# Second phase of a hybrid decoder step: each block's recurrence cut into 27 stages, rounds that mix the stages of neighbouring blocks

## The chip, the cores and the metric

One core of a Trainium2 chip. The metric is the device time of one launch in microseconds (us), the median of the runs shown. Engine names: PE is TensorE (PEld its weight loads), DVE is VectorE, ACT is ScalarE, POOL is GpSimd, SP is the queue that issues the weight DMAs.

## The reference, cut to what matters

One layer of a decoder, for a prompt of 1024 tokens and 8 single-token samples, width 1024. A normed and modulated input goes through `w_in`; three recurrences run side by side on its columns, then `w_out`, a second norm and a SwiGLU network.

```
mod = silu(c) @ w_ada + b_ada                      # sh1, sc1, g1, sh2, sc2, g2
h = rmsnorm(x) * (1 + sc1) + sh1
proj = h @ w_in                                    # HGRN2 | Mamba-2 | RWKV-7 columns
o_hg: S_t = diag(f_t) S_{t-1} + k_t v_t^T, o_t = S_t^T q_t ; rmsnorm per head, * silu(gate)
y_mb: h_t = exp(dt A) h_{t-1} + dt x_t B_t^T, y_t = h_t C_t ; + D x, * silu(z), rmsnorm
o_rw: RWKV-7
x = x + g1 * (concat(o_hg, y_mb, o_rw) @ w_out)
h = rmsnorm(x) * (1 + sc2) + sh2
x = x + g2 * ((silu(h @ w_gate) * (h @ w_up)) @ w_down);  y = rmsnorm(x)
```

Both chunked recurrences must carry a state from one block of 128 tokens to the next.

## The kernel before

There are three stretches. The first phase does the input norm, `w_in` and RWKV-7. The **second phase** runs HGRN2 and Mamba-2 over eight blocks of 128 tokens. The rest is the feed-forward network, with the samples' states in between. Every engine runs its own program, and all programs are written out from one list, `PLAN2` (built around lines 816 to 1010): each item names a piece of work, and each engine does its part of the items in the list's order. An engine never reorders, so a wait in one item holds up all that stands behind it on that engine. Semaphores count finished steps; `step(names, name, b)` gives the count at which step `name` of block `b` is done.

Per block the second phase has these pieces. HGRN2: `hg_logits` (DVE takes the negative magnitude, ACT exp and log), `hg_gate`, `hg_low`, `hg_high` (DVE builds the gates' running sums and differences over 5 levels, ACT exponentiates them), `hg_levels` (DVE multiplies them with keys and queries), `hg_att` (PE transposes, then 192 small matmuls, L1697; DVE masks and adds, `HAS`, `HAT`, `HAD`; ACT copies values, `HVD`), `hg_state` (PE L1705, DVE carries the state, `HSH`, L3008), `hg_o` (PE L1713 and L1718), `hg_sq` (DVE copies and squares, `HT`, PE sums, L1724, ACT inverse root), `hg_out`. Mamba-2: `mb_turn` (PE transposes and two products, DVE `XD`, `CBM`), `mb_decay` (PE running sums, L1754, ACT exp `E2`, DVE 8 subtractions `SEG`, L3088, ACT exp, L2322, DVE `MM`, L3093; POOL scales `XDE` and `CE`), `mb_prod` (PE L1766, L1769, L1772; DVE `YS`, the state `STt`, the gate), `mb_sq` (ACT square, PE sum, L1782, ACT inverse root), `mb_out`.

All of a block's pieces come one after the other, in one fixed order for all blocks, and one item carries the piece's work of all engines. Only `hg_logits`, `hg_gate`, `hg_low`, `hg_high`, `mb_turn`, `hg_levels` of block b+1 are set among the pieces of block b. Between pieces stands work that fills PE:

- in blocks 0 to 2 one quantum of `ada` (8 small matmuls on a 512 KB piece of `w_ada`, L1377; 32 quanta in all), with three transposes of the input, `hg_x`;
- in blocks 3 to 7 dense quanta: one is the product of a 128-wide weight tile with 384 tokens, 24 matmuls (three per contraction tile, L1346 to L1348, high and low parts), or about half of that for `down`. `FILL` puts up to two halves, mostly a whole quantum, behind each of six pieces. Quanta 110 to 117 are the output projection, then comes the second norm (`sum`, `scaled`, `head`, `rest`), and 118 to 139 are gate, up and down of the network. Each needs its weights loaded (SP, three `RAW` buffers), cast on ACT (L1959) and its remainder formed on POOL (L1093), for two slots.

After block 7 come the transposes of the remaining input (`x`), a meeting of all engines (`mark`, `join`), and the network at full pace. All of the work is one stream: what the second phase has not done of the dense quanta is done after it.

Of the kernel before, what the change touches and what calls it, by code (L numbers as in the profile page):

```python
# [39 lines left out]
P = 128  # L40
# [59 lines left out]
HGF_DVE = ['nabs', 'logf', 'diffs', 'factors']  # L100
# [4 lines left out]
MBF_DVE = ['xdt', 'cb']  # L105
MB_DVE = ['seg', 'm', 'y', 'S', 'z', 'out']
MB_PE = ['acum', 'y', 'S', 'ssq']
MB_ACT = ['E2', 'L', 'squared', 'rs']
# [62 lines left out]
def kernel_program(nc, ins, outs):  # L171
# [84 lines left out]
    with ctx:  # L256
# [354 lines left out]
        xb_act = sem("xb_act")  # L611
        hgf_dve = sem("hgf_dve")
        hgf_act = sem("hgf_act")
        mbf_dve = sem("mbf_dve")
        mbf_pe = sem("mbf_pe")
        hg_dve = sem("hg_dve")
# [103 lines left out]

        def XUSE(i):

            return (i - 9) // 2 + 1
# [62 lines left out]
        for b in range(NB):  # L786
            for n, at in (('turn1', b), ('mean', b - 1), ('turn2', b), ('var', b - 1), ('mix', b + 1), ('inv1', b),
# [3 lines left out]
                if 0 <= at < NB:  # L791
# [4 lines left out]
                 'inv2': [('fin_shift', 0)], 'inv3': [('fin_conv', 0), ('hg_logits', 0)], 'inv4': [('pre', 'nabs')],  # L796
# [35 lines left out]
        for item in rw_end:  # L832
# [11 lines left out]
        NOW = {('out', (0, KT - 1)): [('sum', 3), ('pause', 0), ('scaled', (3, 0)), ('scaled', (3, 1)), ('head', 3),  # L844
                                      ('pause', 0), ('rest', (3, 0)), ('rest', (3, 1)), ('pause', 0)]}
# [65 lines left out]
        FILL = {'hg_att': 2, 'mb_decay': 2, 'hg_o': 2, 'mb_prod': 2, 'mb_turn': 2, 'hg_levels': 2}  # L911
        for b in range(NB):
            items = [('hg_att', b), ('hg_state', b), ('mb_decay', b), ('hg_o', b), ('hg_logits', b + 1), ('mb_prod', b),
                     ('hg_sq', b), ('hg_gate', b + 1), ('hg_low', b + 1), ('hg_high', b + 1), ('mb_turn', b + 1), ('mb_sq', b), ('hg_out', b),
                     ('hg_levels', b + 1), ('mb_out', b), ('hg_x', b)]
            for item in items:
                if item[1] == NB or (item[0] == 'hg_x' and b > 2):
                    continue
                PLAN2.append(item)
                if item == ('hg_att', 0):  # L920
                    PLAN2.append(('mb_turn', 0))
                if b > 2:
                    fill(FILL.get(item[0], 0))
                elif item[0] not in ('hg_logits', 'hg_gate', 'hg_low', 'hg_out', 'hg_x') and late:
                    group, part, half = UNITS[QUANTA[late[0]][0]][1]
                    if (part, half) == (0, 0) and group > 1:
                        PLAN2.append(('adt', group - 1))
                    PLAN2.append(('mm', late.pop(0)))
                    if not late:
                        PLAN2.append(('adt', 2))  # L930
# [74 lines left out]
        def _(pool):  # L1005
# [122 lines left out]
            def mb_decay(b):  # L1128
                pool.wait_ge(mbf_dve, step(MBF_DVE, 'xdt', b))
                g.tensor_tensor(XDE[:, :, :], XD[:, :, :], ES[:, b, :].unsqueeze(2).broadcast_to([P, 8, 64]),  # L1130
                                ALU.mult).then_inc(mb_pool, 1)
                pool.wait_ge(mb_act, step(MB_ACT, 'E2', b))
                g.tensor_tensor(CE[:, :, :], E2[:, :, :], XB[5][:, b * BLK:(b + 1) * BLK].unsqueeze(1).broadcast_to([P, 4, P]),
                                ALU.mult).then_inc(mb_pool, 1)
# [31 lines left out]
            for what, arg in PLAN2:  # L1166
                if what == 'mb_decay':
# [110 lines left out]
        def _(pe):  # L1278
# [5 lines left out]
            def turn_x(i, bufs):  # L1284

                b0 = 3 + 2 * (i % 2) if i < 9 else 0
# [11 lines left out]
                for k in range(KT):  # L1298
                    src = bufs[i] if i < 9 else bufs[(i - 9) % 2]
                    last = turn(BK8[b0 + k // 4][:, (k % 4) * P:(k % 4) * P + n], src[0:n, k * P:(k + 1) * P], n)  # L1300
                last.then_inc(x_turned, 1)

            def dense(q, half=None):
# [13 lines left out]
                if q >= QJ and (PREV[q] is None or PREV[q] < QP2):  # L1317
                    pe.wait_ge(x_act, 18)
                    pe.wait_ge(x_dve, 18)
                if c == chunks(u)[0] and half != 1:  # L1320
                    pe.wait_ge(w_hi, SIDX[u] + 1)
                    pe.wait_ge(w_lo, SIDX[u] + 1)
# [344 lines left out]
            def hg(stage, b):  # L1667
# [7 lines left out]
                if stage == 'att':  # L1675
# [3 lines left out]
                    if 0 < b <= 3:  # L1679
                        pe.wait_ge(x_act, 9 + b)  # L1680
                        pe.wait_ge(x_dve, 9 + b)
# [5 lines left out]

# [34 lines left out]
                elif stage == 'sq':  # L1722
# [3 lines left out]
                elif stage == 'x':  # L1726
                    pe.wait_ge(*V('out'))
                    pe.wait_ge(mb_act, step(MB_ACT, 'rs', b))
                    turn_x(9 + b, XTOK2)

            def mb(stage, b):
# [19 lines left out]
                elif stage == 'decay':  # L1751
# [4 lines left out]
                    last.then_inc(mb_pe, 1)  # L1756
                elif stage == 'prod':
                    pe.wait_ge(*V('m'))
# [16 lines left out]
                elif stage == 'sq':  # L1775
# [161 lines left out]
        def _(act):  # L1937
# [65 lines left out]
            def x_half(i, dst, t0):  # L2003
                act.wait_ge(x_turned, i + 1)
                n = BLK if i % 9 < NB else NS
                b0 = 3 + 2 * (i % 2) if i < 9 else 0
                a.copy(dst[:, 0:4, t0:t0 + n], BK8[b0][:, :].rearrange("p (k t) -> p k t", k=4)[:, :, 0:n]).then_inc(
# [49 lines left out]
            def ffn_step(what, arg):  # L2057
# [11 lines left out]
                elif what == 'mixsplit':  # L2069
                    if arg == 0:  # L2070
                        act.wait_ge(ada_turned, 3)
# [176 lines left out]
            def hg(stage, b):  # L2248
# [6 lines left out]
                if stage == 'logits':  # L2255
                    act.wait_ge(hgf_dve, step(HGF_DVE, 'nabs', b))
# [10 lines left out]
                elif stage == 'att':  # L2267
# [10 lines left out]
                elif stage == 'sq':  # L2278
# [29 lines left out]
            def mb(stage, b):  # L2308
# [6 lines left out]
                if stage == 'decay':  # L2315
                    act.wait_ge(*T_('acum'))
# [3 lines left out]
                    last.then_inc(mb_act, 1)  # L2320
                    act.wait_ge(*V('seg'))
                    a.activation(SEG[:, :, :], SEG[:, :, :], ACT.Exp).then_inc(mb_act, 1)  # L2322
                elif stage == 'sq':
                    act.wait_ge(*V('z'))
                    a.activation(T4[:, :, :], YS[:, :, :], ACT.Square).then_inc(mb_act, 1)
                    act.wait_ge(*T_('ssq'))
# [60 lines left out]
            for what, arg in PLAN2:  # L2387
                if what == 'adt':
# [40 lines left out]
        def _(dve):  # L2429
# [88 lines left out]
            def x_half(i, dst, t0):  # L2518
                dve.wait_ge(x_turned, i + 1)
                n = BLK if i % 9 < NB else NS  # L2520
                b0 = 3 + 2 * (i % 2) if i < 9 else 0
                v.tensor_copy(dst[:, 4:8, t0:t0 + n],
                              BK8[b0 + 1][:, :].rearrange("p (k t) -> p k t", k=4)[:, :, 0:n]).then_inc(x_dve, 1)
# [415 lines left out]
            def hg(stage, b):  # L2939
# [11 lines left out]
                if stage == 'logits':  # L2951
                    dve.wait_ge(hg_loaded[b % 2], 16 * (b // 2 + 1))
                    hg_nabs(HN, HB).then_inc(hgf_dve, 1)
# [30 lines left out]
                elif stage == 'att':  # L2984
# [28 lines left out]
                elif stage == 'sq':  # L3013
# [50 lines left out]
            def mb(stage, b):  # L3064
# [11 lines left out]
                if stage == 'turn':  # L3076
                    dve.wait_ge(mbf_pe, b + 1)
# [7 lines left out]
                elif stage == 'decay':  # L3085
                    dve.wait_ge(*A('E2'))
# [3 lines left out]
                    last.then_inc(mb_dve, 1)  # L3090
                    dve.wait_ge(*A('L'))
# [3 lines left out]
                    last.then_inc(mb_dve, 1)  # L3095
                elif stage == 'prod':
                    dve.wait_ge(*T_('y'))
                    mb_skip(YS, lambda t: XB[t][:, cols], lambda t: (M1, M2)[t // 2][:, (t % 2) * P:(t % 2 + 1) * P]).then_inc(mb_dve, 1)
                    dve.wait_ge(*T_('S'))
# [4 lines left out]
                    dve.wait_ge(*V('y'))  # L3104
                    v.tensor_tensor(YS[:, :, :], YS[:, :, :], MIX[:, 2:6, cols], ALU.mult).then_inc(mb_dve, 1)
# [127 lines left out]
            for what, arg in PLAN2:  # L3233
                if what == 'adt':
# [55 lines left out]
```

## Time and profile before

| | |
|---|---|
| time, median of 3 runs | 1798.88 us (1790.7 to 1802.05) |
| profiled execution: span from first to last instruction | 1790.1 us |
| PE, DVE, ACT busy | 89%, 58%, 37% |
| second phase, 609.33 to 979.00 us | 369.67 us, PE busy 289.51 us, granted clock 0.82 |
| network, 1100 to 1790 us | PE busy 95%, granted clock 0.99 |

The profiled execution's own device time isn't on the page; its span lies 0.6 us below the fastest of the three runs. Times within the trace are counted from the span's start. The granted clock is a share of 2.4 GHz, the mean over a stretch.

### The profile page before, as it was taken

The page shows a single profiled execution, that of the slowest core. Times are in us where ns is not written, and L with a number is a line of the kernel's source. Part 1 is how long each engine was busy: PE and PEld are TensorE (multiplying, and loading weights), DVE is VectorE, ACT ScalarE, POOL GpSimd, SP SyncE. Part 2 cuts the span into 40 slices and gives each one's busy share as a digit, 9 for nine tenths or more (in the row PEclk, how much of TensorE's full clock was granted, in tenths as well). Part 3 has the DMA queues.
Part 4 walks back from the last instruction along what each step waited for, and adds up shares of the span by engine and source line. Part 5 has one row for each costly group of instructions (what it writes and reads, how often), then busy time and mean ns, then how long its engine had stood idle before and what let it go on. Part 6 is the DMA issues. An engine that isn't in the chain of part 4 may idle for free.

```text
span 1790.1 us, 32642 instructions
## 1 busy us (share of the span) xinstructions
PE 1594.7 (89%) x13639; PEld 1451.0 (81%) x13639; DVE 1043.3 (58%) x2152; ACT 660.4 (37%) x1133; POOL 249.0 (14%) x331
## 2 busy tenths in 40 slices
PE   4799999889999677777888899989899999999997
PEld 2798888778887443575777899988899999999997
DVE  5513456868554556676765254676665566655554
ACT  2323333223432322343433254343544444433333
POOL 4421111111111200231334300100000000000000
PEclk9899999889999667897998999999999999999999
DMA  8111001101112244321132434544464544564552
GB/s 320 53 48 36 25 25 37 44 33 50 49 43 106 80 164 151 110 86 34 42 89 71 136 117 130 151 121 138 119 200 137 160 122 139 152 176 137 145 151 75
DMA packets 276684, 188.09 MB, mean 105 GB/s; under 512 B 7880, under 2 KB 264377, under 8 KB 275513
## 3 DMA queue, kind: packets, MB, share of 16 engines
q1 hardware_dynamic: 266050, 160.28, 29.8%
q0 software_dynamic: 7536, 22.47, 3.8%
q10 hardware_dynamic: 2950, 3.24, 0.5%
q8 instruction: 109, 1.79, 0.4%
q14 instruction: 39, 0.31, 0.1%
HBM read 172.82 MB, written 13.18 MB: 104 GB/s over the span
## 4 chain that ended last, share of the span: by engine, by line
PE 70%; DVE 17%; ACT 7%; issue 3%; DMA 1%; SPq 0%; POOL 0%; DVEq 0%; ACTq 0%; POOLq 0%
PE bank L1346 16%; PE bank L1347 16%; PE bank L1348 16%; PE bank L1282 3%; PE bank L1368 3%; PE bank L1369 2%; ACT WHI L1959 2%; PE bank L1370 2%; DVE WLO L2442 1%; PE bank L1512 1%; PE bank L1520 1%; PE bank L1522 1%; PE bank L1697 1%; PE bank L1456 1%; PE bank L1377 1%
## 5 line engine op out<-in xcount | busy, mean ns | idle before, releaser
L2442 DVE TENSOR_TENSOR WLO<-RAW,WHI 128x1024 fp32r<-128x1024 f32 (+4 forms) x235 | 247.1, 1052 | 265.1 <-ACT WHI L1959 263.3
L1959 ACT CAST WHI<-RAW 128x1024 fp32r<-128x1024 f32 (+4 forms) x294 | 266.4, 910 | 227.6 <-PE bank L1348 201.0
L1346 PE MATMUL bank<-HAH,WHI 128*128 128x384 f32 (+1 forms) x832 | 277.2, 333 | 12.4 <-DVE HAL L2625 5.9
L1347 PE MATMUL bank<-HAL,WHI 128*128 128x384 f32 (+1 forms) x832 | 273.7, 329 | 0.0
L1348 PE MATMUL bank<-HAH,WLO 128*128 128x384 f32 (+1 forms) x832 | 273.0, 328 | 0.0
L1346 PE MATMUL bank<-MIXR,WHI 128*128 128x384 f32 (+2 forms) x528 | 174.1, 330 | 12.6 <-DVE MIXR L2572 3.8
L1093 POOL TENSOR_TENSOR WLO<-RAW,WHI 128x1024 fp32r<-128x1024 f32 (+1 forms) x59 | 124.6, 2114 | 434.7 <-ACT WHI L1959 434.7
L1346 PEld LDWEIGHTS bank<-HAH,WHI 128*128 128x128 f32 x832 | 159.9, 192 | 16.3 <-issue 15.5
L1347 PE MATMUL bank<-MIXR,WHI 128*128 128x384 f32 (+2 forms) x528 | 171.1, 324 | 0.0
L1348 PE MATMUL bank<-MIXR,WLO 128*128 128x384 f32 (+2 forms) x528 | 171.1, 324 | 0.0
L1347 PEld LDWEIGHTS bank<-HAL,WHI 128*128 128x128 f32 x832 | 159.9, 192 | 0.1
L1348 PEld LDWEIGHTS bank<-HAH,WLO 128*128 128x128 f32 x832 | 159.7, 192 | 0.0
L1346 PE MATMUL bank<-HBH,WHI 128*128 128x320 f32 x416 | 132.2, 318 | 11.2 <-DVE WLO L2442 10.5
L1348 PE MATMUL bank<-HBH,WLO 128*128 128x320 f32 x416 | 129.7, 312 | 0.0
L1347 PE MATMUL bank<-HBL,WHI 128*128 128x320 f32 x416 | 129.6, 312 | 0.0
L1346 PE MATMUL bank<-HHI,WHI 128*128 128x344 f32 x344 | 114.7, 333 | 11.2 <-DVE HLO L2661 7.1
L1346 PEld LDWEIGHTS bank<-MIXR,WHI 128*128 128x128 f32 x528 | 101.4, 192 | 16.7 <-issue 13.8
L1347 PE MATMUL bank<-HLO,WHI 128*128 128x344 f32 x344 | 111.4, 324 | 0.0
L1348 PE MATMUL bank<-HHI,WLO 128*128 128x344 f32 x344 | 111.4, 324 | 0.0
L1368 PE MATMUL bank<-HHI,WHI 128*128 128x344 f32 x280 | 104.6, 373 | 3.7 <-ACT STG L1992 3.7
L1347 PEld LDWEIGHTS bank<-MIXR,WHI 128*128 128x128 f32 x528 | 101.1, 191 | 0.2
L1348 PEld LDWEIGHTS bank<-MIXR,WLO 128*128 128x128 f32 x528 | 101.0, 191 | 0.0
(582 smaller groups left out, 3031.6 us busy)
## 6 DMA issues: line engine op xcount, KB each, us to landing
RAW<-in_w_gate SPq DMA_DIRECT2D x66, 512.0 KB, 3.8
RAW<-in_w_up SPq DMA_DIRECT2D x66, 512.0 KB, 3.8
RAW<-in_w_ada SPq DMA_DIRECT2D x32, 512.0 KB, 4.4
RAW<-in_w_in SPq DMA_DIRECT2D x26, 512.0 KB, 3.8
RAW<-in_w_out SPq DMA_DIRECT2D x24, 512.0 KB, 3.5
RAW<-in_w_down SPq DMA_DIRECT2D x32, 384.0 KB, 3.1
RAW<-in_w_down SPq DMA_DIRECT2D x32, 320.0 KB, 2.8
ADAW<-in_w_ada SPq DMA_DIRECT2D x8, 1024.0 KB, 19.8
```

The costliest lines, as they stand in the source:

```text
L1093: g.tensor_tensor(wlo[:, 0:nk, :], RAW[u % NRAW][:, 0:nk, :], whi[:, 0:nk, :].bitcast(F32), ALU.subtract).then_inc(w_lo, 1)
L1282: return nc.tensor.transpose(out, in_, ident[0:n, 0:n])
L1346: mm(bank[:, 0:w], whi[:, k, :], hi_k, start=(k == 0), stop=False)
L1347: mm(bank[:, 0:w], whi[:, k, :], lo_k, start=False, stop=False)
L1348: last = mm(bank[:, 0:w], wlo[:, k, :], hi_k, start=False, stop=(k == nk - 1))
L1368: mm(bank[:, 0:CH], whi[:, k, :], HHI[:, k, cols], start=(k == 0), stop=False)
L1369: mm(bank[:, 0:CH], whi[:, k, :], HLO[:, k, cols], start=False, stop=False)
L1370: last = mm(bank[:, 0:CH], wlo[:, k, :], HHI[:, k, cols], start=False, stop=(k == KT - 1))
L1377: return mm(bank[32 * a_:32 * a_ + 32, :], CT[:, k, :], w, start=(k == 0 and half == 0), stop=(k == KT - 1), skip_group_check=True)
L1456: mm(BK8[2 + v // 2][:, o:o + w], WL[:, j * P:(j + 1) * P], la[:, v, 0:w], start=True, stop=True)
L1959: a.copy(w_split(i)[0][:, 0:nk, :], RAW[u % NRAW][:, 0:nk, :]).then_inc(w_hi, 1)
L2442: v.tensor_tensor(wlo[:, 0:nk, :], RAW[u % NRAW][:, 0:nk, :], whi[:, 0:nk, :].bitcast(F32), ALU.subtract).then_inc(w_lo, 1)
```

## The change

The stages of a block are cut finer and get semaphores that let them be placed apart: `hg_att` becomes `turn`, `att`, `mask`; `hg_logits` becomes `nabs` and `soft`; `hg_sq` becomes `ho`, `ssq`, `rs`; `mb_turn` becomes `turn`, `xd`; `mb_decay` becomes `acum`, `seg`, `L`, `m`; `mb_prod` becomes `prod`, `y`, `S`; `mb_sq` becomes `sq`, `ssq`. That is 27 stages with the pieces that stay whole. An item's work on one engine thus no longer stands in front of what another item wants from it. Three lists give the order of a round: `AROUND` for blocks 0 to 2, with 13 places for an `ada` quantum, `NROUND` for block 4, with the second norm inside, and `FROUND` for the rest. A round holds stages of block b-1 (`mb_S`, `mb_ssq`, `hg_out`, `mb_out`), of b, of b+1 (`hg_gate`, `hg_low`, `hg_high`) and of b+2 (`hg_nabs`, `hg_soft`). Dense halves come mostly one at a time. The modulation's copy, turn and addition (`adc`, `adt`, `adm`) stand 4, 5 and 7 stages behind the last `ada` quantum of a group. The transposed input uses banks 2 and 7 instead of 0 and 1 for its first three tiles. The mixing of the first 384 tokens waits expressly for blocks 0 to 2.

By the two lists, the work between the sums of squares of neighbouring blocks (`mb_ssq`, L1782) holds, in whole dense quanta, 4 before and 2 after for block 3; 5 and 7.5 for block 4; 6 and 5 for block 5; 6 and 4.5 for block 6; 5 and 4 for block 7. When block 7 is through, quanta up to 139 are done before and up to 136 after. The following engines' meeting stands before quantum 156 in the old list and before quantum 150 in the new one.

```
-        FILL = {'hg_att': 2, 'mb_decay': 2, 'hg_o': 2, 'mb_prod': 2, 'mb_turn': 2, 'hg_levels': 2}
-        for b in range(NB):
-            items = [('hg_att', b), ('hg_state', b), ('mb_decay', b), ('hg_o', b), ('hg_logits', b + 1), ('mb_prod', b),
-                     ('hg_sq', b), ('hg_gate', b + 1), ('hg_low', b + 1), ('hg_high', b + 1), ('mb_turn', b + 1), ('mb_sq', b), ('hg_out', b),
-                     ('hg_levels', b + 1), ('mb_out', b), ('hg_x', b)]
...
+        AROUND = [('mb_ssq', -1), ('mb_S', -1), ('mb_turn', 0), ('hg_levels', 0), ('hg_turn', 0), ('ada', 0), ('hg_att', 0),
+                  ('ada', 0), ('mb_xd', 0), ('hg_out', -1), ('mb_out', -1), ('mb_acum', 0), ('ada', 0), ('ada', 0),
+                  ('hg_mask', 0), ('mb_seg', 0), ('mb_L', 0), ('hg_state', 0), ('hg_x', 0), ('ada', 0), ('ada', 0), ('ada', 0),
+                  ('mb_m', 0), ('hg_o', 0), ('hg_gate', 1), ('ada', 0), ('hg_low', 1), ('ada', 0), ('mb_prod', 0), ('hg_ho', 0),
+                  ('hg_ssq', 0), ('hg_high', 1), ('ada', 0), ('hg_rs', 0), ('hg_nabs', 2), ('mb_y', 0), ('mb_sq', 0),
+                  ('ada', 0), ('hg_soft', 2), ('ada', 0)]
+        FROUND = [('mb_S', -1), ('fill', 2), ('mb_ssq', -1), ('mb_turn', 0), ('hg_levels', 0), ('hg_turn', 0), ('hg_out', -1),
+                  ('mb_xd', 0), ('fill', 1), ('hg_att', 0), ('hg_mask', 0), ('mb_acum', 0), ('mb_seg', 0), ('hg_state', 0),
+                  ('mb_L', 0), ('mb_m', 0), ('mb_out', -1), ('fill', 3), ('hg_o', 0), ('hg_gate', 1), ('mb_prod', 0),
+                  ('hg_low', 1), ('hg_ho', 0), ('fill', 1), ('hg_high', 1), ('fill', 1), ('mb_y', 0), ('mb_sq', 0),
+                  ('hg_nabs', 2), ('fill', 1), ('fill', 1), ('hg_soft', 2), ('hg_ssq', 0), ('hg_rs', 0)]
+        NROUND = [('mb_ssq', -1), ('mb_S', -1), ('mb_turn', 0), ('hg_levels', 0), ('fill', 1), ('hg_turn', 0), ('fill', 1),
+                  ('mb_xd', 0), ('hg_att', 0), ('hg_out', -1), ('mb_out', -1), ('hg_mask', 0), ('mb_acum', 0), ('mb_seg', 0),
+                  ('mb_L', 0), ('hg_gate', 1), ('mb_m', 0), ('hg_state', 0), ('sum', 0), ('scaled', 0), ('hg_o', 0),
+                  ('scaled', 1), ('hg_low', 1), ('hg_ho', 0), ('mb_prod', 0), ('hg_ssq', 0), ('head', 0), ('hg_high', 1),
+                  ('rest', 0), ('rest', 1), ('hg_nabs', 2), ('mb_y', 0), ('go', 0), ('mb_sq', 0), ('hg_rs', 0), ('hg_soft', 2),
+                  ('fill', 1)]
...
+        for b in range(NB + 1):
+            for stage, ahead in (AROUND if b < 3 else NROUND if b == 4 else FROUND):
+                at = b + ahead
+                if stage == 'ada':
+                    ada_quantum()
+                elif stage == 'fill':
+                    if b < NB and ('mb_out', 2) in PLAN2:
+                        fill(ahead)
+                elif stage in ('sum', 'head'):
+                    fill(len(QUANTA))
+                    PLAN2.append((stage, 3))
```

## Rows read from the trace of the kernel before

**Rows 1.** The page: busy time by engine; clock in 40 slices (tenths).
```profile
PE 1594.7 (89%) x13639; PEld 1451.0 (81%) x13639; DVE 1043.3 (58%) x2152; ACT 660.4 (37%) x1133; POOL 249.0 (14%) x331
...
PEclk9899999889999667897998999999999999999999
```

**Rows 2.** Windows: from:to, length, busy us (instructions) of PE, PEld, DVE, ACT, POOL, clock.
```profile
609.33:979.00 369.67, 289.51 (x3434) 224.38 (x3434) 245.84 (x646) 130.80 (x230) 101.60 (x70) 0.82 0.31 97
```

**Rows 3.** Windows of the second phase's single rounds, and one of the network.
```profile
609.33:648.68 39.35, 30.90 (x420) 17.34 (x421) 25.25 (x80) 10.30 (x20) 9.88 (x15) 0.68 0.51 167
...
691.23:725.69 34.46, 26.49 (x408) 14.81 (x408) 23.58 (x78) 10.89 (x21) 3.21 (x3) 0.80 0.59 190
...
835.24:883.38 48.14, 42.46 (x460) 37.73 (x459) 34.42 (x83) 21.07 (x37) 16.83 (x9) 0.93 0.18 53
...
1060.00:1100.00 40.00, 39.66 (x236) 38.48 (x234) 19.91 (x32) 17.14 (x30) 0.00 (x0) 0.99 0.43 126
```

**Rows 4.** Timeline of PE: the sum of squares of all eight blocks, idle before it.
```profile
643.53 1.16 PE L1782 MATMUL bank<-T,ones 128*128 128x128 f32 x8 [1.29 <-ACT T L2325]
...
719.97 1.16 PE L1782 MATMUL bank<-T,ones 128*128 128x128 f32 x8 [0.44 <-ACT T L2325]
...
772.38 1.16 PE L1782 MATMUL bank<-T,ones 128*128 128x128 f32 x8 [3.53 <-ACT T L2325]
...
830.08 1.16 PE L1782 MATMUL bank<-T,ones 128*128 128x128 f32 x8 [1.72 <-ACT T L2325]
...
878.20 1.16 PE L1782 MATMUL bank<-T,ones 128*128 128x128 f32 x8 [3.46 <-ACT T L2325]
...
931.48 2.07 PE L1782 MATMUL bank<-T,ones 128*128 128x128 f32 x8 [4.89 <-ACT T L2325]
...
975.15 1.76 PE L1782 MATMUL bank<-T,ones 128*128 128x128 f32 x8 [3.50 <-ACT T L2325]
```

**Rows 5.** Chain that ended last, 640 to 743 us: start, us, what.
```profile
642.30 3.79 DMA RAW<-in_w_ada
...
700.71 2.17 DVE SEG L3088 x8
702.90 1.06 ACT SEG L2322
...
738.47 4.31 DVE HAL L2625
```

**Rows 6.** Timeline of PE: first dense matmul of the phase, and one 4 us later.
```profile
742.92 0.66 PE L1346 MATMUL bank<-HAH,WHI 128*128 128x384 f32 x1 [5.95 <-DVE HAL L2625]
...
744.02 0.52 PE L1346 MATMUL bank<-HAH,WHI 128*128 128x384 f32 x1
...
748.09 0.33 PE L1347 MATMUL bank<-HAL,WHI 128*128 128x384 f32 x1
```

**Rows 7.** Chain that ended last, second norm, 798 to 823 us.
```profile
800.06 2.38 DVE SSA L2589
...
806.08 4.33 DVE MIX L2546 x8
...
810.44 4.16 ACT HAH L2044 x8
...
814.63 4.32 DVE HAL L2560 x8
...
822.82 0.62 PE bank L1346
```

**Rows 8.** Waits from 609 to 979 us: total, times, longest.
```profile
ACT WHI L1959 <- PE bank L1348: 76.2, 20, 7.0
```

**Rows 9.** Timeline of ACT and DVE: a weight cast; one DVE operation twice.
```profile
847.26 1.04 ACT L1959 CAST WHI<-RAW 128x1024 fp32r<-128x1024 f32 x1 [6.98 <-PE bank L1348]
...
868.99 0.42 DVE L2922 TENSOR_TENSOR HK<-HF,HB 128x256 f32<-128x256 f32 x1
...
922.24 2.50 DVE L2922 TENSOR_TENSOR HK<-HF,HB 128x256 f32<-128x256 f32 x1
```

More of the change, by code:

```diff
@@ new lines, in kernel_program, with turn_group, ada_quantum @@
+        turning = []
+        def turn_group():
+            for due in turning:
+                due[0] -= 1
+            while turning and turning[0][0] <= 0:
+                PLAN2.append(turning.pop(0)[1])
+        def ada_quantum():
+            if late and not turning:
+                group, part, half = UNITS[QUANTA[late[0]][0]][1]
+                PLAN2.append(('mm', late.pop(0)))
+                if (part, half) == (KT - 1, 1):
+                    turning.extend([[4, ('adc', group)], [5, ('adt', group)], [7, ('adm', group)]])
@@ new lines, in kernel_program @@
+        PLAN2 += [('hg_nabs', 1), ('hg_soft', 1)]
+        for b in range(NB + 1):
[9 more added lines that the diff above has]
+                    PLAN2.append((stage, 3))
+                elif stage in ('scaled', 'rest'):
+                    PLAN2.append((stage, (3, ahead)))
+                elif stage == 'go':
+                    assert ffn[0][0] == 'stop', ffn[0]
+                    ffn.pop(0)
+                elif 0 <= at < NB and (stage, at) != ('hg_levels', 0):
+                    PLAN2.append((stage, at))
+                    turn_group()
@@ L931, in kernel_program @@
+        assert not turning
         assert not late
@@ L1319, in dense @@
                     pe.wait_ge(x_dve, 18)
+                if QP2 <= q < QJ and PREV[q] is None and half != 1:
+                    pe.wait_ge(x_act, 12)
+                    pe.wait_ge(x_dve, 12)
                 if c == chunks(u)[0] and half != 1:
@@ L1674, in hg @@
                 HB = HB2[b % 2]
-                if stage == 'att':
+                if stage == 'turn':
                     pe.wait_ge(hgf_dve, step(HGF_DVE, 'factors', b))
@@ L2266, in hg @@
                     a.activation(HD[:, :, :, :], HD[:, :, :, :], ACT.Exp).then_inc(hgf_act, 1)
-                elif stage == 'att':
+                elif stage == 'turn':
                     act.wait_ge(*T_('turned'))
@@ L2387, in _ @@
             for what, arg in PLAN2:
-                if what == 'adt':
+                if what == 'adc':
                     ada_act(arg)
```

121 lines of the change are left out of this document (57 added, 64 removed).

## The prediction

> **What bounds the kernel now.** I read the page first: PE is busy 89% of the span, no other engine over 58%, and the clock row shows where PE is not at its pace: it stands at 9 and 10 tenths in the last half, and dips to 6, 7 and 8 in slices 14 to 22 [rows 1]. That is the second phase. The windows put numbers to it: in its 369.67 us PE is busy 289.51, DVE 245.84, ACT 130.80, at a mean clock of 0.82 [rows 2]. The network's stretch beside it has PE busy 39.66 of 40 us at 0.99 [rows 3]. So the phase loses time twice: 369.67 - 289.51 = 80.2 us of idle PE, and busy time at a low clock; 289.51 x 0.82 = 237 us is what its work would take at full clock. No engine fills the phase; it is bound by handovers. The chain of waits shows them: DVE subtracts for 2.17 us, ACT exponentiates for 1.06, in turn, with PE waiting for the end of that [rows 5], and PE's wait before the sum of squares, up to 4.89 us, comes in each of the eight blocks [rows 4]. After 979 us nothing of this remains, so what the phase saves goes to the end of the span one for one, except for dense work that it leaves for later.
>
> The markers that I use are the sums of squares of the blocks [rows 4]. Up to block 2's: 719.97 - 609.33 = 110.6 us. Then 52.4, 57.7, 48.1, 53.3 and 43.7 us for blocks 3 to 7, which is 365.8 us in all.
>
> **Rounds 0 to 2 (`ada`).** Nothing is added or removed: the same instructions on each engine, plus a few semaphore steps, at nothing. What moves is the order. A round's PE time was 26.5 us at clock 0.80, in a round of 34.5; DVE's was 23.6 [rows 3]. In the new order the subtraction on DVE runs while PE has the state product and `ada` quanta; the products `mb_prod` come after `hg_o` and two more quanta, and the sums of squares of block b come in the next round, behind three quanta. Walking the list with the measured durations, the DVE stream runs without a hole from `mb_m` to `hg_nabs`, and PE's own time is the longer one. I take PE's 26.5 us plus 3.5 for what is left: one is the load of a `w_ada` piece, on which the chain once stood 3.79 us [rows 5], because 11 quanta a round now come in groups of up to three, and there are three `RAW` buffers. 3 x 30 = 90 us instead of 110.6. Bounds: 26.5 (no waits at all) and 34.5 (nothing gained) a round.
>
> **Round 3.** Dense work now starts only after `mb_out` of block 2, which stands late, some 20 us into DVE's round of 23.6. Then ACT casts 3072 columns (estimate 3.1 us, from 1.04 for 1024 [rows 9]) with DVE waiting for it, and DVE forms the remainder in 4.31 us [rows 5]; the express wait makes that a chain. 20 + 3.1 + 4.3 = 27.5, then two quanta. A quantum is 24 matmuls; 236 took 40 us [rows 3], so 4.1 us. Round 3: 36 us instead of 52.4, with 2 quanta done instead of 4. The first dense matmul, at 742.92 us before [rows 6], comes at about 609 + 90 + 28 = 727.
>
> **Round 4 (norm).** PE's recurrence work is what round 5 shows: 42.46 x 0.93 = 39.5 us at full clock [rows 3], less six quanta of 4.1, or 15 us. Before the norm stand some 9 of these and six quanta, 24.6; with 2 of waiting, 36 us. The norm is a chain: from the last squares at 799.5 to the end of the remainder at 814.63 + 4.32 it took 19.4 us [rows 7]; of that DVE's additions of 2.38 would be less without POOL beside them, and the 4.33, 4.16 and 4.32 stay. PE has only `hg_o`, `mb_prod` and `hg_ssq` under it, 6 us. I take 19, plus a quantum and a half behind it, 6: 61 us instead of 57.7, but with 7.5 quanta instead of 5. Nothing is gained on this chain, since no stage of it moves.
>
> **Rounds 5 to 7.** Work of 15 us plus 5, 4.5 and 4 quanta: 35.5, 33.5 and 31.4 at full clock. DVE had 34.4 us in round 5 [rows 3], with less in the others. I take 38, 36 and 33, that is 2 to 2.5 above PE's work, instead of 48.1, 53.3 and 43.7.
>
> **Sum.** 90 + 36 + 61 + 38 + 36 + 33 = 294 us instead of 365.8: 71.8 earlier. Three quanta less are done by then, 3 x 4.1 = 12.3 us that come after: 59.5. The walk leaves out two things that rows show. The first dense matmuls after a wait take 0.66 and 0.52 us, 0.33 later [rows 6], so the first quantum took some 6 instead of 4.1; one such start in each of five rounds is 9.5 us. And DVE takes 2.50 us for what takes 0.42 otherwise, when POOL forms a remainder at the same time [rows 9]: this stays, and once a round it now falls on the chain, since DVE has fewer holes: 2.1 x 2.4 = 5. 59.5 - 14.5 = **45 us**. What a sum like this misses lies on both sides: neither at all gives 59.5, and a further 2.5 us of waiting a round gives 25; 65 is the end above, with the ada rounds at 28. Span 1790.1 - 45 = 1745; the median stood 8.8 us above this span, and I keep that: 1798.9 - 45 = **1754 us**.
>
> The later meeting of all engines moves before quantum 150, with less PE work between mark and meeting (two quanta of `down`, 4 us at most). POOL's outputs were issued long before, so I cost it at nothing; if POOL or DVE is behind it costs what they are late by, at most some 3 us. The change of banks and the three modulation items are nothing by themselves: the 4 to 7 stages between them replace PE's and DVE's waits for one another.
>
> **A view from the other side.** Work at full clock: 237 - 12.3 = 225 us. The forecast gives the phase 369.7 - 12.3 - 45 = 312.4 us; at a mean clock of 0.85 PE would be busy 265 us and idle 47, of the 80 now. DVE's 246 us are 79% of it.
>
> **The rivals.**
>
> *The dense bursts are broken up and the clock falls (slower).* Now the dense work comes in whole quanta; after the change a half, 2 us, stands between small matmuls and waits, and the ada rounds, where PE works in pieces of 1 us, ran at 0.68 [rows 3]. Place: rounds 3 to 7. With 47 us idle the phase costs 225 / c + 47: at c = 0.85 it is the forecast, at 0.725 it equals the old 357.4 (the quanta set aside), and from there on it is a loss; at 0.68 it is 378, 21 us slower: 1820. Against it: PE's idle stretches get shorter by the same change, and the clock was higher in the rounds in which PE idled least (0.93 in round 5, with 42.46 of 48.14 busy [rows 3]). The Trainium skill has a rule that speaks for this rival (TensorE: Matmul & The Clock Gate, section "A second HAM failure mode: psum-queue depth-cycling"): where PE idles a little between groups of matmuls that go to different banks, the clock goes back and forth and throughput drops. By the rule the halves, which cycle through three banks, would bring such a drop; the trace doesn't decide it, for it has no round with single halves. Chance 0.08.
>
> *ACT's queue takes back half.* ACT stands in its weight casts waiting for PE to release a slot: 76.2 us over 20 waits, up to 7.0 [rows 8, 9]. Behind such a cast are now `hg_soft`, `mb_sq`, `hg_rs` of other blocks. If each of the 27 casts in the phase makes one stage late by its 1.04 us [rows 9], that is 28 us: a gain of 17, 1782. For it: the dense weights have two slots, before and after. Against it: a cast is released when PE ends the very half that stands before it. Chance 0.17.
>
> *The order doesn't bound it.* If the pace is set by the weight stream or by DVE once its holes are filled, the PE waits come back under other names; gain within 8 us, 1795. Against it: DVE busy 66% and ACT 35% of the phase [rows 2], and twice the pace of weights in the network, without PE waiting. Chance 0.07.
>
> **How the numbers follow.** Forecast (gain 25 to 65) 0.64, more than 65 0.04, ACT's queue 0.17 (gain 8 to 25), no effect 0.07, clock 0.08. The range leaves out what lies beyond 65, the clock's case and most of "no effect": 1734 to 1791. A difference below 1% (18 us) is about what a measurement of this kernel can't tell from none. Faster by more: 0.64 + 0.04 + 0.10 of ACT's case = 0.78. Within 1%: the rest of ACT's case, most of "no effect", a little of the clock's: 0.13. Slower: 0.09.
>
> **What would show it.** PE idle in the phase down from 80 to about 47 us; clock from 0.82 to about 0.85, most of it in rounds 0 to 2; sums of squares of blocks 2, 3, 4, 7 at about 699, 735, 796 and 903 us; the wait before them (3.5 us, [rows 4]) gone; the first dense matmul at 727; the chain of the norm as long as before. Wrong would be: ada rounds still 34 us or more, a clock under 0.75 in rounds 5 to 7, DVE waiting for PE in the middle of a round while a bank waits to be emptied, or a wait of PE at the meeting.

## The result, and the profile after

The changed kernel takes 1767.03 us (median; 1764.87 to 1776.19) against 1798.92 before. The ratio is 0.9845, interval 0.982 to 0.987: faster by 1.3 to 1.8%, 23 to 32 us. The profiled execution's span is 1764.4 us, 25.7 below the one before. The forecast was 1754 us, a gain of 45, in a range up to 1791.

The page of the changed kernel, first part and clock; the second phase is slices 14 to 21:

```profile
span 1764.4 us, 32641 instructions
...
PE 1586.9 (90%) x13639; PEld 1448.9 (82%) x13639; DVE 1056.0 (60%) x2154; ACT 659.9 (37%) x1133; POOL 247.0 (14%) x329
...
PEclk9899999888999679788898999999999999999998
```

The instructions are the same in number on PE; only their places differ. Windows of the changed kernel: the whole phase up to the last state's transposes, then rounds 0 to 2, round 3, round 4 in three pieces (up to the norm's last squares, the norm, behind it), rounds 5, 6 and 7. Columns as in [rows 2]; behind the clock stand the DMA engines' busy share and GB/s.

```profile
609.33:931.59 322.26, 268.75 (x3363) 210.27 (x3363) 251.62 (x650) 124.46 (x220) 95.78 (x65) 0.83 0.35 107
...
609.33:698.47 89.14, 75.53 (x1221) 45.52 (x1221) 66.42 (x222) 30.59 (x60) 16.30 (x21) 0.80 0.65 212
698.47:736.88 38.41, 29.95 (x368) 24.32 (x368) 31.65 (x80) 15.03 (x23) 11.86 (x6) 0.73 0.24 66
...
736.88:779.44 42.56, 34.89 (x382) 32.59 (x380) 34.97 (x67) 16.70 (x29) 18.78 (x10) 0.96 0.30 86
779.44:799.02 19.58, 11.74 (x80) 6.18 (x81) 14.98 (x33) 7.87 (x15) 2.34 (x1) 0.56 0.18 51
799.02:806.92 7.90, 7.90 (x36) 7.90 (x37) 6.32 (x23) 3.19 (x6) 0.70 (x1) 0.78 0.01 2
806.92:846.53 39.61, 36.19 (x437) 31.83 (x436) 31.37 (x70) 19.41 (x34) 16.16 (x9) 0.96 0.22 65
846.53:888.82 42.29, 38.43 (x425) 32.38 (x424) 33.24 (x89) 16.46 (x31) 12.23 (x10) 0.84 0.16 45
888.82:925.00 36.18, 33.07 (x412) 28.69 (x412) 27.32 (x61) 12.27 (x21) 14.25 (x8) 0.91 0.28 82
```

PE idles 322.26 - 268.75 = 53.5 us in the phase instead of 80.2 [rows 2], and the clock went from 0.82 to 0.83 only. PE's waits in the phase, before and after:

```profile
PE bank L1782 <- ACT T L2325: 21.1, 8, 4.9
PE bank L1724 <- DVE HT L3017: 13.4, 5, 9.0
PE bank L1766 <- DVE MM L3093: 9.2, 3, 3.1
PE bank L1697 <- ACT HKT L2270: 7.7, 4, 3.2
```

```profile
PE bank L1758 <- DVE HSH L3053: 7.0, 3, 4.2
PE bank L1423 <- DMA RAW<-in_w_ada: 6.1, 5, 2.3
PE bank L1326 <- DVE MIX L3105: 5.5, 1, 5.5
PE bank L1326 <- DVEq L688: 5.2, 1, 5.2
...
PE bank L1825 <- ACT T L2370: 2.0, 2, 1.5
PE bank L1809 <- DVE MM L3139: 1.5, 1, 1.5
```

The four waits that led the list, 51 us, are nearly gone: 3.5 us of them are left. What leads now are waits for a state, for a `w_ada` piece, for the last block's `MIX` at the phase's end, and the barrier at the phase's start, which was there before. The sums of squares (L1825 now; its wait of up to 4.89 us [rows 4] is gone in six of eight blocks):

```profile
698.47 1.16 PE L1825 MATMUL bank<-T,ones 128*128 128x128 f32 x8 [0.53 <-ACT T L2370]
...
736.88 1.05 PE L1825 MATMUL bank<-T,ones 128*128 128x128 f32 x8
...
806.92 1.05 PE L1825 MATMUL bank<-T,ones 128*128 128x128 f32 x8
...
925.00 1.05 PE L1825 MATMUL bank<-T,ones 128*128 128x128 f32 x8
931.59 0.69 PE L1326 MATMUL bank<-ident,STt 128*128 128x128 f32 x2 [5.53 <-DVE MIX L3105]
```

| block's sum of squares | before | forecast | after |
|---|---|---|---|
| 2 | 719.97 | 699 | 698.47 |
| 3 | 772.38 | 735 | 736.88 |
| 4 | 830.08 | 796 | 806.92 |
| 7 | 975.15 | 903 | 925.00 |

The transposes of the state came at 979.10 us before and come at 931.59: 47.5 us, less three quanta of 4.1 left over, 35.2 us. But the span is only 25.7 us shorter. 9.5 us are lost **after** the phase. From the transposes of the last input tile to the sum of the norm behind the first `down` groups, the kernel before took 1265.68 - 1019.37 = 246.3 us, the changed one 1241.42 - 974.45 = 267.0, with five `down` quanta more, each of half a quantum's size (10.3 us): 10.4 too many. PE's waits in the changed kernel at the end of that stretch:

```profile
1213.51 0.41 PE L1392 MATMUL bank<-MIXR,WHI 128*128 128x384 f32 x1 [2.59 <-DVE WLO L2488]
...
1227.89 0.39 PE L1392 MATMUL bank<-HBH,WHI 128*128 128x320 f32 x1 [3.19 <-DVE WLO L2488]
...
1241.42 1.65 PE L1441 MATMUL bank<-SSA,ones 128*128 128x384 f32 x2 [4.50 <-DVE SSA L2634]
```

The longest wait for squares there was 1.47 us before. DVE and ACT beside them:

```profile
1220.61 1.22 DVE L3239 TENSOR_TENSOR SB<-SB,SW 128x1024 f32<-128x1024 f32 x1
1221.87 1.23 DVE L3240 TENSOR_TENSOR SW<-SB,SV 128x1024 f32<-128x1024 f32 x1
1223.12 1.22 DVE L3241 TENSOR_REDUCE SY<-SW 128x16 f32<-128x1024 f32 x1
1224.38 0.62 DVE L2561 SCALAR_TENSOR_TENSOR XTA<-bank,MOD,XTA 128x384 f32<-128x384 f32 x1
```

```profile
1229.78 1.28 ACT L1989 ACT_TABLE_LOAD   x1
1233.35 0.27 ACT L2418 ACTIVATE SRSV<-bank,CST 128x16 f32<-128x16 f32 x1 [2.28 <-PE bank L1881]
1233.65 0.21 ACT L2420 ACTIVATE SRSV<-SRSV 128x16 f32<-128x16 f32 x1
1233.89 1.28 ACT L1989 ACT_TABLE_LOAD   x1
```

L3239 to L3241 and L2418 are steps of the samples' states (`sm4b`, `sr12`). Three of them stand 3.7 us in front of the emptying of a bank (`XTA`), behind `down` quanta that PE had got through in 2.1 us each; the other takes two table loads (1.28 us each) and a wait in front of a weight cast. The samples' steps are placed by counting dense work from the meeting on. The meeting moved from quantum 156 to 150, and all 37 steps moved with it.

### The profile page after: what moved, and what is told of

It is laid out like the page before. It is cut to its first block, busy times and chain, and to the rows that moved or that the text cites. A ratio compares the mean times of both kernels' runs of the same rounds, so it can differ in the third digit from the quotient of the medians.

```text
span 1764.4 us, 32641 instructions
## 1 busy us (share of the span) xinstructions
PE 1586.9 (90%) x13639; PEld 1448.9 (82%) x13639; DVE 1056.0 (60%) x2154; ACT 659.9 (37%) x1133; POOL 247.0 (14%) x329
## 4 chain that ended last, share of the span: by engine, by line
PE 69%; DVE 19%; ACT 5%; issue 4%; DMA 2%; SPq 0%; POOL 0%; DVEq 0%; ACTq 0%; POOLq 0%
PE bank L1392 16%; PE bank L1393 16%; PE bank L1394 16%; PE bank L1326 3%; PE bank L1414 3%; PE bank L1415 2%; PE bank L1416 2%; ACT WHI L2002 1%; DVE WLO L2488 1%; PE bank L1423 1%; PE bank L1558 1%; PE bank L1566 1%; DVE HD L3023 1%; PE bank L1568 1%; PE bank L1797 1%
## 5 line engine op out<-in xcount | busy, mean ns | idle before, releaser
L1392 PE MATMUL bank<-HAH,WHI 128*128 128x384 f32 (+1 forms) x832 | 275.9, 332 | 13.6 <-DVE HAL L2605 4.2
L1392 PE MATMUL bank<-HBH,WHI 128*128 128x320 f32 x416 | 132.9, 319 | 13.1 <-DVE WLO L2488 11.6
```

Source lines behind the costliest of these rows:

```text
L1392: mm(bank[:, 0:w], whi[:, k, :], hi_k, start=(k == 0), stop=False)
```

## The experiments

All are compared with the kernel before in alternating runs; the changed kernel's ratio is 0.9845. A run's difference from the changed kernel is taken from the ratios, times 1797 us. Single profiles scatter: the second phase starts between 605.6 and 612.8 us in them (610.31 in the changed kernel), and round 0 takes 29.6 to 35.2 us from there in kernels with the same order, at clocks from 0.60 to 0.87. So the medians decide, and profiles are read for stretches.

**Old order in rounds 0 to 2.**

```
+        AOLD = [('hg_turn', 0), ('hg_att', 0), ('hg_mask', 0), ('ada', 0), ('hg_state', 0), ('ada', 0), ('mb_acum', 0), ('mb_seg', 0),
+                ('mb_L', 0), ('mb_m', 0), ('ada', 0), ('hg_o', 0), ('ada', 0), ('hg_nabs', 1), ('hg_soft', 1), ('mb_prod', 0),
...
-            for stage, ahead in (AROUND if b < 3 else NROUND if b == 4 else FROUND):
+            for stage, ahead in (AOLD if b < 3 else NROUND if b == 4 else FROUND):
```

> Blocks 0 to 2 in the old order, written with the new stages (all stages of a block one after the other, one ada quantum between pieces); blocks 3 to 7 as changed. My theory: the ada rounds took 110.6 us up to block 2's sum of squares before and 89.1 after, because the handovers are covered there; with the old order they go back to about 110, and the kernel to 1767 + 21 = 1788 us. Rival: the gain of these rounds is not the order of the stages but the modulation's three items set apart and the banks of the transposed input, which stay: then it stays at 1767, within 5 us.

1793.78 us, ratio 0.9991 (0.9973 to 1.001): 26 us slower than the changed kernel. The rival (banks and the modulation's items) is out. The window up to block 2's sum of squares, and from PE's waits (sum, count, longest):

```profile
609.33:729.67 120.34, 87.58 (x1222) 49.50 (x1222) 71.51 (x234) 30.04 (x58) 16.30 (x21) 0.68 0.49 160
```

```profile
PE bank L1818 <- DVE MM L3148: 9.2, 3, 3.1
```

The wait for `MM` is back, in the same 9.2 us as before, and the clock falls from 0.80 to 0.68. The same matmuls keep PE busy 87.6 instead of 75.5 us, and from where the phase starts it idles 29.3 instead of 12.6. My rewriting isn't the old list to the letter (the last `ada` quanta bunch up): counted from where its phase starts, 612.79, it took 116.9 us where the kernel before took 110.6, so the 26 us are an upper value for the order; the profiles before and after put it at 22. The scatter doesn't hide this: counted in the same way, the twelve kernels with the new order (the changed one and eleven of the runs below) took 83.5 to 95.2 us for these three rounds.

**Old order in rounds 3 to 7.**

```
-            for stage, ahead in (AROUND if b < 3 else NROUND if b == 4 else FROUND):
+            for stage, ahead in (AROUND if b < 3 else FOLD0 + FOLD if b == 3 else FOLD if b < NB else []):
```

`FOLD` is the old order in the new stages with `('fill', 2)` behind each piece; the norm's steps go back to where `NOW` had them.

> Blocks 0 to 2 as changed, blocks 3 to 7 in the old order with whole quanta between pieces and the norm as before; the meeting of all engines then stands before quantum 156, as before. My theory: rounds 3 to 7 gave 28.7 us less 12.3 for three quanta left over, 16 us; undone they cost 16, less some 8 if the earlier meeting costs that: 1775 us. Rival (all of the gain is made in the ada rounds, and what the dense rounds show is lost again after them): 1767 or less. Rival (the dense rounds are the main thing): 1785 or more.

1784.67 us, ratio 0.9936 (0.9917 to 0.9956): 16 us slower by the ratio, 17.6 by the medians. That is the figure of the second rival (1785 or more) and not mine (1775). The list also takes the meeting back to its old place, so the right comparison is the run with the late meeting below (0.9788), which it shares: against that the order, as I rewrote it, is worth 0.0148, 27 us and not the 16 of my figure. From block 2's to block 7's sum of squares it took 262.5 us for 26 quanta, the changed kernel 226.5 for 23; the difference less 12.3 is 23.7. The kernel before had 255.2: here too my list is 7 us slower than the old one. So both halves of the phase gained: some 22 us in the first three rounds, some 16 in the others by the profiles, which were then handed back in part.

**Whole quanta instead of halves.**

```
-                  ('mb_xd', 0), ('fill', 1), ('hg_att', 0), ('hg_mask', 0), ('mb_acum', 0), ('mb_seg', 0), ('hg_state', 0),
-                  ('mb_L', 0), ('mb_m', 0), ('mb_out', -1), ('fill', 3), ('hg_o', 0), ('hg_gate', 1), ('mb_prod', 0),
-                  ('hg_low', 1), ('hg_ho', 0), ('fill', 1), ('hg_high', 1), ('fill', 1), ('mb_y', 0), ('mb_sq', 0),
...
+                  ('mb_xd', 0), ('hg_att', 0), ('hg_mask', 0), ('mb_acum', 0), ('mb_seg', 0), ('hg_state', 0),
+                  ('mb_L', 0), ('mb_m', 0), ('mb_out', -1), ('fill', 4), ('hg_o', 0), ('hg_gate', 1), ('mb_prod', 0),
+                  ('hg_low', 1), ('hg_ho', 0), ('fill', 2), ('hg_high', 1), ('mb_y', 0), ('mb_sq', 0),
```

> As changed, but in the rounds of blocks 3 to 7 the dense halves come in pairs, a whole quantum at a time, at four places of a round instead of seven. The theory of the broken-up bursts: with whole quanta the clock in rounds 5 to 7 rises above 0.90 and the kernel gains 5 us or more, 1762 or less. My theory: the halves cover handovers and the clock follows PE's idle time, so whole quanta leave 1 to 2 us more waiting a round, 1772, clock the same or lower.

1775.63 us, ratio 0.988 (0.9835 to 0.9926): 6 us slower, not faster; the interval reaches to the changed kernel's. Rounds 5 to 7 in windows: whole quanta, the changed kernel, and the kernel before:

```profile
810.44:937.27 126.83, 106.16 (x1283) 93.34 (x1283) 94.50 (x218) 48.89 (x86) 43.51 (x25) 0.91 0.20 58
```

```profile
806.92:925.00 118.08, 107.69 (x1270) 92.90 (x1270) 91.93 (x218) 48.14 (x85) 42.65 (x25) 0.90 0.22 63
```

```profile
830.08:975.15 145.07, 123.81 (x1345) 110.27 (x1345) 93.97 (x224) 57.00 (x100) 52.42 (x29) 0.91 0.21 62
```

The clock is the same, the idle time twice as long, 20.7 instead of 10.4 us; the work differs by half a quantum. The halves don't break the clock, and in this profile they cover handovers. But the other part of my theory falls too: PE's idle share is 9% here in the changed kernel, 16% with whole quanta and 15% in the kernel before, and the clock is 0.90, 0.91 and 0.91. In these rounds the clock does not follow the idle time, and what the change gained there is idle time alone.

**The meeting late again.**

```
+        fill(len(QUANTA), True)
         if ffn[0][0] == 'stop':
             ffn.pop(0)
         samples_at = len(PLAN2)
```

> As changed, but the meeting of all engines stands before quantum 156 as in the kernel before; until its mark the weight remainders are formed on POOL. From the transposes of the last input tile to the sum of squares of the third norm PE idled 7.8 us more than before. My theory: the earlier meeting hands the remainders to DVE sooner and starts the samples' DVE work sooner, and that costs these 8 us: 1759. Rival: the loss comes from the three quanta that are done later, whatever the meeting: 1767, within 3 us.

1759.58 us, ratio 0.9788 (0.9752 to 0.9824): 10 us faster than the changed kernel. The phase itself is as before (state's transposes at 931.85 us), the stretch behind it takes 258.3 instead of 267.0 us. So the loss is tied to the meeting's place. Three runs ask what of it costs.

**Early meeting, remainders on POOL longer; late meeting, remainders on DVE sooner.**

```
-                LO_BY[arg] = 'pool' if at < samples_at else 'dve'
+                LO_BY[arg] = 'pool' if at < PLAN2.index(('half', (QJ + 6, None))) else 'dve'
```

> As changed, with the early meeting, but the weight remainders stay on POOL until quantum 156. The late meeting alone gave 10 us. If what the early meeting costs is that DVE takes over the remainders 6 quanta sooner (with twice the DVE work per quantum while it empties banks and sums squares): this run gives the same 10 us, 1757. If it is the meeting or the samples' earlier start: 1767.

The complement takes `dve_from`, the place behind the last input tile, in the same line and the late meeting's `fill`.

> The late meeting (before quantum 156), but DVE takes over the remainders where the changed kernel has it, behind the last transposed input tile. The complement of the run before: if the remainders on DVE are the cost, 1767; if the meeting and the samples' start are, 1757. Both at once (each half) would give 1762 in both runs.

1764.83 us, ratio 0.982 (0.9802 to 0.9838), and 1756.2 us, ratio 0.9767 (0.9741 to 0.9793). The remainders' engine makes 4 us at most, and in the late case none in DVE's disfavour. My theory of them falls. The first run's trace has the same waits as the changed kernel's: 3.19 us for a remainder, here at 1228.93, and 4.50 for squares.

**Early meeting, late samples.**

```
+            if item[0] == 'half' and item[1][0] < QJ + 6:
+                spent = 0
             if samples and spent >= 12 * FCW[0]:
```

> As changed, with the early meeting, but the samples' steps begin only at quantum 156, as in the kernel before and in the run with the late meeting. The remainders on POOL or DVE made no difference there. If the earlier samples are what costs (their DVE steps fall on other quanta: PE waited 14.1 us for weight remainders and 4.5 for squares instead of 9.4 and 1.5): 1758. If it is the meeting itself, or the weight slots: 1767.

1750.27 us, ratio 0.9746 (0.9725 to 0.9767): 18 us faster than the changed kernel, more than the late meeting gave. The stretch behind the phase takes 253.3 us, PE's waits for remainders on DVE sum to 6.5 us instead of 14.1, and the one for squares is back at 1.47 us:

```profile
1223.31 0.91 PE L1443 MATMUL bank<-SSA,ones 128*128 128x384 f32 x2 [1.47 <-DVE SSA L2636]
```

The early meeting costs nothing; the samples' steps on the wrong quanta do. In this run, as in the kernel before and with the late meeting, the plan has each of the 37 steps at the same quantum, from 157 on; in the changed kernel the first stands at 151. The stretch from the transposes of the last input tile to the sum of squares bears it out over all profiles with the changed kernel's 23 quanta in rounds 3 to 7:

| meeting | samples' steps | profiles | stretch, us |
|---|---|---|---|
| early | early | 7 | 265.0 to 268.0 |
| late | late | 3 | 257.3 to 258.3 |
| early | late | 2 | 253.3, 253.3 |

So in the profiles late samples are worth 13.6 us in this stretch, of which 1.7 are given back behind it, against the 18 us by the ratio. This profile also ended the phase 4 us sooner, where nothing was changed: that is scatter. That the early meeting with late samples beats the late meeting is at the edge of the intervals by the ratios (0.004); the profiles put it at 5 us.

**An early mixing in block 3.** A list for this block in which `mb_out` of block 2 stands behind `hg_out`, and the mixing's cast and remainder behind the attention:

```
+        MROUND = [('mb_ssq', -1), ('mb_S', -1), ('mb_turn', 0), ('hg_levels', 0), ('hg_turn', 0), ('hg_out', -1), ('mb_out', -1),
+                  ('mb_xd', 0), ('hg_att', 0), ('fill', 0), ('hg_mask', 0), ('mb_acum', 0), ('mb_seg', 0), ('hg_state', 0),
+                  ('fill', 2), ('mb_L', 0), ('mb_m', 0), ('fill', 1), ('hg_o', 0), ('hg_gate', 1), ('mb_prod', 0),
+                  ('hg_low', 1), ('hg_ho', 0), ('fill', 1), ('hg_high', 1), ('fill', 1), ('mb_y', 0), ('mb_sq', 0),
+                  ('hg_nabs', 2), ('fill', 1), ('hg_soft', 2), ('hg_ssq', 0), ('hg_rs', 0)]
```

> As changed, but block 3 gets a round of its own: mb_out of block 2 stands right behind hg_out, the mixing's cast and remainder right behind the attention, and dense halves start behind the state product. In the changed kernel the first dense matmul of the phase waits for mb_out of block 2 at 717.0 us, the cast and a remainder that ends at 723.3. My theory: that chain starts some 8 us earlier and PE's holes of round 3 (8.5 us idle, clock 0.73) are filled with a quantum more: 5 us less, 1762. Rival (DVE bounds round 3, busy 31.7 of 38.4 us, so it doesn't matter where its 4 us of mixing stand): 1767, within 2 us.

1752.31 us, ratio 0.9761 (0.9732 to 0.9791): 15 us faster, within 7 us or so, three times what I had expected. Timeline of PE, first dense matmul, here and in the changed kernel:

```profile
709.49 0.69 PE L1397 MATMUL bank<-HAH,WHI 128*128 128x384 f32 x1
```

```profile
725.71 0.66 PE L1392 MATMUL bank<-HAH,WHI 128*128 128x384 f32 x1 [1.77 <-POOL WLO L1137]
```

It comes 16 us sooner, but this profile has block 2's sum of squares 3.7 us sooner too, where nothing was changed; counted from there it is 12.5 us. My estimate was 8; I think it forgot that PE, too, had the whole attention between. The norm's sum (768.0 instead of 783.1) comes 11.3 us sooner by the same count, and the next rounds keep it: from block 2's to block 7's sum of squares it takes 214.9 us instead of 226.5.

**The norm in halves.** New semaphores hand four of eight tiles from scaling to cast and from cast to remainder; `hg_low`, `hg_ho`, `hg_ssq`, `hg_high` stand behind it.

```
+                    if n == 3 and k == KT // 2:
+                        last.then_inc(n3_hi, 1)
+                        act.wait_ge(n_h, 7)
```

> As changed, but the second norm's scaling, cast and remainder go in two halves of four contraction tiles, handed over half by half, and the stages hg_low, hg_ho, hg_ssq, hg_high, hg_nabs and mb_y of this round stand behind them. The chain took 4.33 + 4.16 + 4.33 us with PE idle 4.2 us at its end and at half clock in it. My theory: the chain of three becomes one of two, 12.8 to 8.7 us, and the kernel gains 4 us, 1763. Rival (the stages put behind the norm come late and hold up the next round by as much): 1767.

1759.34 us, ratio 0.9794 (0.9779 to 0.9809): 9 us faster. The chain that ended last, here:

```profile
783.63 2.22 DVE MIX L2599 x4
785.87 2.14 ACT HAH L2094 x4
788.04 4.33 DVE HAL L2618 x8
792.50 0.66 PE bank L1394
```

From the sum of squares to the first matmul behind it, 11.8 us instead of 15.9. That is 4.1 of the 9. From block 2's to block 7's sum of squares the profile gains 6.9 us; what lies above the 4.1, I think, is less waiting behind the norm, but no run separates it.

**No remainder on POOL.**

```
-                LO_BY[arg] = 'pool' if at < samples_at else 'dve'
+                LO_BY[arg] = 'dve'
```

> As changed, but POOL forms no weight remainder; DVE does all (1.22 us each instead of 2.36 on POOL). My prediction set 5 us for DVE operations of the chain that take 2.5 instead of 0.4 us beside POOL. If that is right and the holes in DVE's stream take the 30 remainders (in all about 30 us over rounds 3 to 7, of which DVE is busy 180 of 226), this run is within 3 us of 1767 or faster. If DVE is the bound of these rounds, as its share of 0.8 suggests, it costs half of what it adds: 1780.

1779.33 us, ratio 0.9902 (0.9882 to 0.9923): 10 us slower, the figure given for DVE as the bound. But the trace doesn't show that reason. From block 2's to block 7's sum of squares DVE was busy 179.9 of 226.5 us in the changed kernel and is busy 171.3 of 238.0 here, with 28 remainders (29.9 us) more. Its other work fell from 179.9 to 141.4 us with no remainder on POOL beside it. One such operation, in the changed kernel and here:

```profile
L2634 DVE TENSOR_TENSOR SSA<-SSA,SQT 128x384 f32<-128x384 f32 x7 | 11.3, 1617 | 2.9 <-ACT SQT L2068 2.8
```

```profile
L2634 DVE TENSOR_TENSOR SSA<-SSA,SQT 128x384 f32<-128x384 f32 x7 | 3.9, 550 | 0.1
```

What came in its place is a wait. DVE now stands in front of a remainder until ACT has cast the weight, 20 times, and all that stands behind it in DVE's order stands too:

```profile
DVE WLO L2488 <- ACT WHI L2002: 46.6, 20, 7.3
```

So the run exchanges one price for another. The remainders on POOL cost DVE 38.5 us of busy time in these rounds; how much of that lies on PE's path, where the prediction has 5 us, stays open, as no run has the remainders on DVE at places where the casts are done.

**All together,** with the late meeting, and with late samples instead:

> The late meeting, the early mixing of block 3 and the halved norm together. Each alone, by the ratio to the kernel before: 0.979, 0.976, 0.979, against 0.9845 of the changed kernel. The three lie in different stretches (after 975 us, 698 to 737, 783 to 807), so by my theory they add up: 0.9845 - 0.006 - 0.008 - 0.005 = 0.965, 1734 us. Rival (parts of these gains are the same PE idle time, handed on): 1745 or more.

> The early mixing of block 3 and the halved norm, with the early meeting and the samples' steps from quantum 156 on. The late samples alone gave 0.9746 and the late meeting 0.979, the three together with the late meeting 0.970 instead of the 0.965 of the sum. By my theory the late samples are worth as much here as the late meeting or 0.004 more: 0.966 to 0.970, 1738 to 1743 us. Rival (the two are the same within what is measured): 0.970, 1743.

1743.22 us, ratio 0.9699 (0.9681 to 0.9717), and 1738.74 us, ratio 0.968 (0.9655 to 0.9704). In the first the three gains make 26 of the 34 us that they made singly, near the rival's 1745 and not my 1734; in the second 30 of 42. The second lies in the range that I gave, but 0.9699 and 0.968 can't be told apart by their intervals; the 5 us that the profiles show between the late meeting and the late samples speak for it. From block 2's to block 7's sum of squares the mixing and the norm gained 11.6 and 6.9 us singly, 14.2 and 11.3 together: whether the missing part is the same idle time or scatter, no run separates. The last is the fastest version: 3.2% under the kernel before, 1.7% under the changed one.

## Why the prediction was right, point by point

The direction and the mechanism were right: the waits for handovers went, and the kernel gained. The time lies in the range. The gain was less than forecast: by the spans 25.7 instead of 45 us, of which 9.8 are missing in the phase and 9.5 behind it. The medians stand 31.9 us apart, since the changed kernel's lies 2.6 above its profiled span and not the 8.8 that I kept. That part of the agreement is luck.

- **Rounds 0 to 2:** 90 us forecast, 89.1 measured; with the old order the gain is gone. The size is right, but the agreement to 1 us is luck: kernels with the same order took 83.5 to 95.2, and within this profile round 0 took 34.0 us from its own start at clock 0.60, the next 24.7 and 29.5.
- **Round 3:** 36 forecast, 38.4 measured; first dense matmul at 727, measured 725.71. The chain (mixing waits for `mb_out`, ACT casts 2.75 us, DVE 3.36) is as described.
- **Round 4:** 61 forecast, 70.0 measured, the largest miss. Not the norm: 19 forecast, 19.6 measured. The term that was mis-sized is the part before it, 36 forecast, 42.6 measured, with PE busy 34.9 at 0.96. The work was right; I gave it 2 us of waiting and it had 7.7, of which 3.3 for a bank that DVE emptied late (`XTA`) and 2.0 of issue.
- **Rounds 5 to 7:** 38, 36, 33 forecast, 39.6, 42.3, 36.2 measured. Round 6 ran at clock 0.84.
- **What the walk left out:** up to block 7's sum of squares the walk was short by 21.7 us (903 forecast, 925.00 measured), and behind it the wait of 5.53 us for `MIX` made 2.6 more than before; 14.5 had been set aside, so 9.8 are missing. Idle time was 53.5 instead of 47, clock 0.83 instead of 0.85. One of the set-aside terms doesn't follow from its own words: POOL beside DVE "once a round" over five rounds is 2.1 x 5 = 10.4 us and not 2.1 x 2.4 = 5, which would have made the forecast 1759. The run without remainders on POOL shows 38.5 us of DVE's time for it, of which no run gives the part on PE's path.
- **The later meeting "at nothing":** this step failed. I looked at who is late at the meeting, where nobody is, and not at what is placed by counting from it. The runs showed the samples' steps in its place: 12 to 18 us are won back when they alone are put where they were.
- **The clock rival (0.08):** refuted by the result and by the run with whole quanta. It wanted a clock of 0.68 to 0.725; rounds 5 to 7 ran at 0.90, and at 0.91 before. The Trainium skill (TensorE: Matmul & The Clock Gate, "A second HAM failure mode: psum-queue depth-cycling") tells of a kernel in which small idles between groups of matmuls in changing banks made the clock go back and forth and cost throughput. In all three kernels here the dense quanta go through the same three banks in turn, so the run tests the length of a group, a half or a whole quantum, and not the banks; that length made no difference to the clock.
- **"About 0.85, most of it in rounds 0 to 2":** there it is so, 0.70 before and 0.80 after. Against the clock rival the prediction held that shorter idle stretches bring a higher clock; in rounds 5 to 7 they did not.
- **ACT's queue (0.17):** not what is missing. PE waited for no weight cast in the phase, and 2.9 us in all for ACT; ACT's own waits for a slot fell from 76.2 us [rows 8] to 40.8. Through DVE it can still have cost something (DVE waited 8.2 us for `SGF` of ACT in rounds 3 to 7); no run tests that.
- **"The order doesn't bound it" (0.07):** refuted by the two runs with the old orders. Its part about DVE, whose holes would be filled, is not shown: DVE was busy 79% of rounds 3 to 7, and where it was given more to do it was busy less and waited more.

## What to carry to other kernels

When an item in an in-order plan is used as the origin for placing others, moving it moves them all; ask of a moved marker what counts from it. A phase bound by handovers is helped by cutting items at their waits and putting another block's work between; look then for the first item of the next kind of work, since where it waits for one late stage, the whole round before it is spoiled (some 12 us here, for three stages moved up). A chain of passes by two or three engines over one tensor is worth halving before anything is put under it (4 us here). And work moved to an engine with time to spare costs what it waits for at its place in that engine's order, whatever its own length.

## What the runs showed of the hardware that was not expected

The same matmuls of rounds 0 to 2 kept PE busy 75.5 us at clock 0.80 in the new order and 87.6 at 0.68 in the old one. Over all profiles it is 70.6 to 81.2 us for the new order, and 84.6 and 87.6 for the old, so there covering handovers paid more than their length. But PE's idle share alone doesn't give the clock. Rounds 5 to 7 show it, and round 0 of two kernels with the same order there, the changed one and the one with the late meeting, from where their phase starts: 8% idle at 0.60, and 21% idle at 0.87, with the first 4.4 us longer for the same work.

```profile
610.31:644.34 34.03, 31.30 (x412) 17.91 (x412) 21.39 (x69) 10.25 (x20) 9.92 (x15) 0.60 0.62 207
```

```profile
610.35:639.99 29.64, 23.34 (x411) 13.81 (x411) 20.97 (x59) 9.58 (x19) 9.88 (x15) 0.87 0.68 234
```

So two profiles of one order can differ by 5.6 us in round 0 alone (29.6 to 35.2).

The same operations of DVE in rounds 3 to 7 took 179.9 us with 28 remainders on POOL beside them and 141.4 without; those on 384 elements in two inputs (`SSA`) went from 1.62 to 0.55 us in the mean.
